# Second mixer of a two-layer backbone: eleven context copies on ScalarE, small rows ahead of the large ones, residual rows loaded late

## What is computed

```python
m = (mod_in @ mod_w[layer] + mod_b[layer])[:, None, :]
sh1, sc1, g1, sh2, sc2, g2 = jnp.split(m, 6, axis=-1)
h = modulate(rms_norm(x, norm1_g[layer]), sh1, sc1)
...
for di, rev in enumerate((False, True)):
    ...
    yc_d, h_ctx = s5_scan(u_c, lam_bar, b_bar, c_mat, h0, rev, need_ctx)
    yl_d, _ = s5_scan(u, lam_bar, b_bar, c_mat, h_ctx, rev, True)
    y = y + yl_d
...
z = jax.nn.gelu(t.reshape(t.shape[:2] + (dm,)))
val, gt = jnp.split(z @ glu_w + glu_b, 2, axis=-1)
return val * jax.nn.sigmoid(gt)
...
x = x + g1 * y
```

## Time and profile before

| | us |
|---|---|
| median of 3 runs | 2512.29 |
| lowest and highest run | 2508.5, 2512.55 |
| the profiled execution | 2506.16 |
| its span, first to last instruction | 2504.4 |

### The profile page before, as it was taken

The page is one execution under the profiler, slowest core; times in us unless marked ns, Lnnn a source line. Parts: engine busy times, 40 slices in busy tenths (PEclk is TensorE's granted clock), DMA queues, the critical chain, the costliest instruction groups (busy, mean ns, idle before and its releaser), DMA issues. The chain is left out here.

```text
span 2504.4 us, 40476 instructions
## 1 busy us (share of the span) xinstructions
PE 2143.6 (86%) x11989; PEld 1189.9 (48%) x11990; DVE 1092.3 (44%) x2311; ACT 509.8 (20%) x945; POOL 433.9 (17%) x359
## 2 busy tenths in 40 slices
PE   5889999997999999999999816699789999988874
PEld 3765444744544444444444405354444444444442
DVE  8853365944543333333333338942532222222222
ACT  3443233611121111111111125220221111100000
POOL 1000000002012222222222210000122222232332
PEclk9999999998999999999999968799799999999997
DMA  9971002003799999999999669830499999899996
GB/s 358 386 265 46 34 34 84 1 1 131 264 346 355 354 358 357 359 351 350 355 358 358 202 158 329 275 146 0 160 404 375 361 363 358 274 390 372 385 385 207
DMA packets 173622, 666.72 MB, mean 266 GB/s; under 512 B 37666, under 2 KB 48898, under 8 KB 129882
## 3 DMA queue, kind: packets, MB, share of 16 engines
q1 hardware_dynamic: 121410, 564.71, 58.7%
q0 software_dynamic: 36160, 64.84, 11.0%
q10 hardware_dynamic: 15960, 35.96, 4.1%
HBM read 617.29 MB, written 86.09 MB: 281 GB/s over the span
## 5 line engine op out<-in xcount | busy, mean ns | idle before, releaser
L1518 PE MATMUL banks_l<-slotw_l,xTw_l 128*128 128x512 f32 x800 | 358.2, 601 | 27.7 <-issue 27.7
L1529 PE MATMUL banks_l<-slotn_l,xTn_l 128*64 128x256 f32 x2816 | 325.0, 383 | 34.5 <-issue 34.5
L1529 PEld LDWEIGHTS banks_l<-slotn_l,xTn_l 128*64 128x64 f32 x2816 | 212.0, 137 | 178.9 <-issue 104.8
L1518 PEld LDWEIGHTS banks_l<-slotw_l,xTw_l 128*128 128x128 f32 x800 | 148.5, 191 | 239.3 <-issue 239.3
L1568 PE MATMUL banks_l<-slotn_l,late_l 128*64 128x512 f32 x704 | 189.9, 615 | 19.6 <-DVE late_l L1356 17.9
L1547 PE MATMUL banks_l<-slotw_l,late_l 128*128 128x512 f32 x400 | 191.8, 602 | 15.4 <-DVE late_l L1338 15.4
L977 POOL DMA_INDIRECT xgw_l<-moe_h,idxw_l x58 | 60.6, 1045 | 741.0 <-PE banks_l L1463 367.1
L1005 POOL DMA_INDIRECT moe_acc<-late_l,idxn_l x88 | 151.2, 1718 | 190.5 <-DMA moe_acc<-late_l,idxn_l 172.5
L937 POOL IOTA slotw_l<- 128x1 f32 x2 | 0.3, 140 | 729.1 <-POOLq L69 431.3
L1335 DVE TENSOR_TENSOR late_l<-late_l,banks_l 128x256 f32<-128x256 f32 x50 | 21.0, 421 | 240.2 <-ACT late_l L1107 240.2
L556 PE MATMUL ps_a<-W_a,hT_a 128*128 128x512 f32 x288 | 124.9, 595 | 0.0
(11 more groups left out here) (433 smaller groups left out, 3235.0 us busy)
## 6 DMA issues: line engine op xcount, KB each, us to landing
slotn_l<-in_exp_w_gate SPq DMA_DIRECT2D x88, 1024.0 KB
slotn_l<-in_exp_w_up SPq DMA_DIRECT2D x88, 1024.0 KB
slotn_l<-in_exp_w_down SPq DMA_DIRECT2D x88, 1024.0 KB, 12.1
slotw_l<-in_exp_w_gate SPq DMA_DIRECT2D x50, 1024.0 KB
slotw_l<-in_exp_w_up SPq DMA_DIRECT2D x50, 1024.0 KB
slotw_l<-in_exp_w_down SPq DMA_DIRECT2D x50, 1024.0 KB
w_p<-in_mod_w SPq DMA_DIRECT2D x12, 2048.0 KB, 15.4
W_a<-in_ar_w_in SPq DMA_DIRECT2D x5, 2048.0 KB, 9.4
```

The costliest lines, as they stand in the source:

```text
L1518: last = pe.matmul(pGU_w, xT_w[b % 2][:, k, :], wgu[0][b % WIDE_RING][:, :, k, :], start=(k == 0), stop=(k == KD - 1))
L1529: last = pe.matmul(pGU_n[H * side:H * side + H, b % 2], xT_n[b % 2][:, k % 4, H * (k // 4):H * (k // 4) + H], w[:, :, k, P * side:P * side ...
```

## The change

The edits are all in `s5_mixer`. Of the 16 backward context copies, ScalarE takes 11, as a third piece per half block; VectorE keeps those of `hb` 2, 5, 8, 11 and 14 (`DVE_CTX`). Sweeps and copies are no longer interleaved stage by stage: for each block VectorE does its remaining copies and then all four stages. ScalarE's queue begins with the small rows. The residual copies from `X` are gone; instead, `parts[0]` is loaded into `x` while the gated products begin, and `parts[1]` into the free lower part of `XS` (`XR`) after the last state product, and VectorE adds the two within unit 0. The three modulation buffers change places, so that the first one is free when the rows are normalised, and its load goes out there. Output weights 3 and 4 wait for two modulation products less. There are 57 memsets.

```diff
-        w = [v.rearrange("p (k n) -> p k n", k=HK) for v in (ZU[:, 0], ZU[:, 1], XS[:, SG * NCL:])]
+        w = [v.rearrange("p (k n) -> p k n", k=HK) for v in (XS[:, SG * NCL:], ZU[:, 0], ZU[:, 1])]
+        XR = XS[:, 0:NL * D].rearrange("p (m d) -> p m d", m=NL)
...
+        DVE_CTX = (2, 5, 8, 11, 14)
+
+        def evicted(hb):
+            return 3 * (hb + 1) - ctx_copied(hb)
+
+        def ctx_copied(hb):
+            return sum(k <= hb for k in DVE_CTX)
...
             for hb in range(R_ACT, NHB):
-                if hb == 4:
-                    sp.wait_ge(S['x_sum'], SL)
-                    for m in range(NL):
-                        for hh in range(2):
-                            sp.dma_start(x[hh * 64:hh * 64 + 64, m, :], X[0:64, 2 * m + hh, :]).then_inc(S['xres_in'], 16)
...
-            sp.wait_ge(S['mod_mm'], LATE)
+            sp.wait_ge(S['mod_mm'], LATE - 2)
...
+            for m in range(NL):
+                for hh in range(2):
+                    sp.dma_start(x[hh * 64:hh * 64 + 64, m, :], tile_rows(parts[0], m, hh)).then_inc(S['xres_in'], 16)
             glu_half(1)
+            sp.wait_ge(S['o_mm'], NB)
+            for m in range(NL):
+                for hh in range(2):
+                    sp.dma_start(XR[hh * 64:hh * 64 + 64, m, :], tile_rows(parts[1], m, hh)).then_inc(S['xres_in'], 16)
...
+            act.wait_ge(S['xn_done'], XN_DVE)
+            act.wait_ge(S['xn_act'], SL - XN_DVE)
+            act.dma_start(w[0], mod_weights(io, *MOD_LATE[0], 0)).then_inc(m_in[0], 16)
...
-            act.wait_ge(S['xres_in'], 16 * 8)
-            for n in range(3):
+            for n in range(1, 3):
                 act.dma_start(w[n], mod_weights(io, *MOD_LATE[n // 2], n % 2)).then_inc(m_in[n], 16)
...
+                if hb not in DVE_CTX:
+                    act.activation(VH[64:P, 0:NCC, :, gs].rearrange("p c a g -> p g a c"), v_of(hb)[64:P, :, :, 0:NCC], ACT.Copy)\
+                       .then_inc(S['va_done'], 1)
...
-            dve.wait_ge(S['xres_in'], 16 * 8)
-            for hb in range(NHB):
-                dve.wait_ge(S['va_done'], 2 * hb + 1)
-                dve.tensor_copy(VH[64:P, 0:NCC, :, 4 * hb:4 * hb + 4].rearrange("p c a g -> p g a c"), v_of(hb)[64:P, :, :, 0:NCC])\
-                   .then_inc(S['vd_done'], 1)
-                if 2 <= hb < 14:
-                    b, third = divmod(hb - 2, 3)
-                    sweep(b, third)
-                    if third == 2:
-                        sweep(b, 3)
-            for b in range(4, NB):
+            dve.wait_ge(S['xn_act'], SL - XN_DVE)
+            for b in range(NB):
+                for hb in (2 * b, 2 * b + 1):
+                    if hb in DVE_CTX:
+                        dve.wait_ge(S['va_done'], evicted(hb - 1) + 1)
+                        dve.tensor_copy(VH[64:P, 0:NCC, :, 4 * hb:4 * hb + 4].rearrange("p c a g -> p g a c"), v_of(hb)[64:P, :, :, 0:NCC])\
+                           .then_inc(S['vd_done'], 1)
                 for stage in range(4):
                     sweep(b, stage)
...
-            for _ in range(50):
+            for _ in range(57):
...
-            dve.wait_ge(S['xres_in'], 16 * 8)
...
+                if u == 0:
+                    dve.wait_ge(S['xres_in'], 16 * 16)
+                    for t in range(NL):
+                        done(dve.tensor_tensor(x[:, t, :], x[:, t, :], XR[:, t, :], ALU.add))
+                    done.wait()
...
-            pe.wait_ge(S['va_done'], 2 * NHB)
-            pe.wait_ge(S['vd_done'], NHB)
+            pe.wait_ge(S['va_done'], evicted(NHB - 1))
+            pe.wait_ge(S['vd_done'], ctx_copied(NHB - 1))
```

More of the change, by code:

```diff
@@ L2088, in s5_mixer, with tile_rows @@
         XN_DVE, R_ACT = 5, 2
+        DVE_CTX = (2, 5, 8, 11, 14)
[3 more added lines that the diff above has]
+            return sum(k <= hb for k in DVE_CTX)
+        def tile_rows(part, m, hh):
+            return part.rearrange("(m h c) d -> m h c d", m=NL, h=2)[m, hh, 0:NCL, :]
         CTX_OPS, STEPS = 4 * 4, NCL // 2 - 1
@@ L2178, in _ @@
         def _(act):
+            for s in range(2):
+                act.dma_start(vec[:, 2 * s:2 * s + 2], io['modrow'][1, s, 0:2 * D].rearrange("(a g j) -> g a j", a=2, j=SI)).then_inc(S['vec_in'], 16)
+            act.dma_start(vec[:, 4], io['norm1_g'][1].rearrange("(g j) -> g j", j=SI)).then_inc(S['vec_in'], 16)
             for j in range(2):
@@ L2181, in _ @@
                    .then_inc(x_in[j], 16)
-            for s in range(2):
-                act.dma_start(vec[:, 2 * s:2 * s + 2], io['modrow'][1, s, 0:2 * D].rearrange("(a g j) -> g a j", a=2, j=SI)).then_inc(S['vec_in'], 16)
-            act.dma_start(vec[:, 4], io['norm1_g'][1].rearrange("(g j) -> g j", j=SI)).then_inc(S['vec_in'], 16)
             act.dma_start(lam[:, 0].rearrange("p a b g -> p (a b g)"), io['s5_l8']).then_inc(S['l8_in'], 16)
@@ L2334, in sweep @@
                         dve.wait_ge(S['up'], n)
-                    dve.wait_ge(S['va_done'], 4 * (b + 1))
-                    dve.wait_ge(S['vd_done'], 2 * (b + 1))
+                    dve.wait_ge(S['va_done'], evicted(2 * b + 1))
+                    if ctx_copied(2 * b + 1):
+                        dve.wait_ge(S['vd_done'], ctx_copied(2 * b + 1))
                     dve.tensor_tensor(a, even, factor(0, 0, NPAIR, g), ALU.mult).then_inc(S['up'], 1)
@@ L2472, in _ @@
                 if hb >= 4:
-                    pe.wait_ge(S['va_done'], 2 * (hb - 3))
-                    pe.wait_ge(S['vd_done'], hb - 3)
+                    pe.wait_ge(S['va_done'], evicted(hb - 4))
+                    if ctx_copied(hb - 4):
+                        pe.wait_ge(S['vd_done'], ctx_copied(hb - 4))
                 for g in range(4):
```

## The result

| | before | after |
|---|---|---|
| median, first comparison (11 runs each) | 2505.49 | 2517.3 |
| median, second comparison (35 and 12 runs) | 2506.35 | 2512.87 |
| ratio, first comparison | | 1.0037, 95% 1.0023 to 1.0050 |
| ratio, second comparison | | 1.0029, 95% 1.0016 to 1.0042 |
| the profiled execution | 2506.16 | 2505.95 |

The ratio is not the quotient of two medians; it and its interval are what counts. The change makes the kernel slower by 0.3 to 0.4%, by the two ratios 7 to 9 us, where a gain of 0.7 us was forecast. The forecast time, 2511.6 us, and its range up to 2516.5 were set around the 2512.29 us of three runs of before; the 2505.49 of the same kernel here is 6.8 us lower.

What follows compares the result with a forecast made beforehand. VectorE's work and the DMA engines compete before the first fill, with VectorE only 2.76 us behind the last modulation product; the fill at 1605.65 against 1606.36 gave -0.7 us, 2511.6 from 2512.29, range 2506 to 2516.5.

Steps and rivals of the forecast that it cites:

- the chain from the copies to the fill: Second mixer: sweeps end 7.6 us earlier, modulation chain shifts 1.9 later, so the first fill starts at 1605.65 against 1606.36.
- Rivals 1 to 3: 1: shift 0, 2509.7, 15%; 2: modulation chain takes whole delay, 2515.1, 20%; 3: VectorE bound, 7.6 kept, 2504.7, 7%.
- I take 0.1, the end that this cover leaves, and keep 2 as the upper: Last x pair sharing turns with three V matrices: 0 to 3.1 us more, taken as 0.1, upper 2.
- The small rows' move: Head of ScalarE's queue: small rows cost the same 6 us of turns early or late, so 0 gained.
- the third pair lands as before: x loads: with the same packets ahead, the third pair isn't moved and the last sum still starts at 1493.60: 0.
- Rival 4: x loads: the last x pair loses turns, +2 us on all, 2513.6 us; chance 8%.
- The gated products keep their distance to it if TensorE catches up: After the first fill: TensorE's lag grows by 2.7 us, but it has 4.9 us to catch up over some 32.
- Cost 0; without it 2.7: Gated products behind the fill: cost 0 us if TensorE catches up, 2.7 us if it doesn't.
- ScalarE's third piece: Context copies: third piece 0.45 us like the second, group 1.77, ScalarE's total 26.1 us against VectorE's 32.45.
- the residual rows: Late loads in by 1668 to 1681, four adds of 4.9 us in unit 0 covered by VectorE's waits: cost 0.
- the relaxed wait of the output weights 3 and 4: SyncE's queue: may go after six products instead of eight, but stands behind block 7's Toeplitz load: does nothing.
- what the residual edit frees: SyncE's queue: 2 MB of copies fewer ahead of V matrices, but V products wait for VectorE's U columns: cost 0.

Runs made afterwards that it cites:

- 9: Kernel before with only the copies changed (11 of 16 on ScalarE) and output weights of blocks 5 to 7 ahead of the GLU weights: mixer 298.47 us, ratio 1.0003.
- 10: Changed kernel with x rows ahead of small rows, V matrices held until the x sums are done, GLU weights behind output weights: mixer 299.01 us, ratio 1.0002.
- 4: Changed kernel with the first half of the GLU weights behind the output weights of blocks 5 to 7: mixer 301.99 us, ratio 1.0012.
- 2: Changed kernel with small rows behind two x loads again and V matrices 4 to 6 held until all x sums are done: mixer 302.37 us, ratio 1.0019.
- 1: Changed kernel with only the small rows put back behind the first two x loads of ScalarE's queue: mixer 304.99 us, ratio 1.0029.
- 6: Kernel before with only the residual edit: late loads and adds, modulation buffers rotated, V matrices 4 to 6 not held: mixer 300.09 us, ratio 1.0011.
- 3: Kernel before with only the copies changed, 11 of 16 on ScalarE and sweeps whole: mixer 301.20 us, ratio 1.0019.

## Why the prediction was wrong

The copies' part can be read without the rest in experiments 9 and 10. Forecast times of before's trace are turned into times from its start:

| step | forecast | 9 | 10 | after |
|---|---|---|---|---|
| last x sum | +32.3 | +32.48 | +32.26 | +36.63 |
| first sweep | +62.1 | +62.13 | +61.91 | +66.29 |
| first level | +94.6 | +95.12 | +94.90 | +99.26 |
| Toeplitz block 0 | +90.9 | +91.31 | +91.10 | +95.46 |
| fourth modulation load issued | +96.6 | +96.84 | +96.68 | +100.71 |
| last modulation product ends | +144.3 | +144.01 | +144.61 | +147.53 |
| first fill | +144.4 | +144.15 | +144.75 | +147.68 |
| fill to first gated product | 39.2 | 39.19 | 39.13 | 41.95 |

**Right: the chain from the copies to the fill.** Sweeps 7.6 us earlier: the first level came 7.2 (9) and 7.4 (10) earlier. Toeplitz products 3.3 later behind the copy of group 14: in after that copy stands at 1554.24 and the first block at 1554.93. The clock had fallen by then; these are windows of after, columns as above:

```profile
1551.00:1552.00 1.00, 0.00 (x0) 0.00 (x0) 1.00 (x2) 0.94 (x2) 0.00 (x0) 0.98 0.99 418
1553.00:1554.00 1.00, 0.00 (x0) 0.00 (x0) 0.96 (x2) 0.00 (x0) 0.00 (x0) 0.50 1.03 434
```

TensorE's last V product began at 1548.25, and block and product took 5.2 us at that clock (issue of the next load at 1560.18; 5.6 in the forecast). The load's late issue cost the chain 1.9 and not 5.5: the end of the last product moved by 1.7 to 2.3. And the fill stood at -0.95 and -0.35 where -0.7 was forecast, against the product and not against VectorE, which had to wait 6.3 and 7.1 us. Rivals 1 to 3 fall with this: the delay was neither absorbed nor passed on whole, and 6.3 to 7.1 us of VectorE's gain were lost.

**Wrong: "I take 0.1, the end that this cover leaves, and keep 2 as the upper".** The last sum came 4.3 us late, and 3.0 us of it reached the mixer's end (4 against 10; 2 against after and its repetition gives 2.4 and 3.3). The step failed in three places. The small rows' move was priced at 0 by counting turns, and the count was right: by the third x sum ScalarE's queue had moved 1213 packets before and 1206 after. But turns need a start too, and the small rows moved no packet of x in the first 4 us where 64 had gone before; the stretch of the earlier trace rows lies 14 us further on and doesn't show the start. This half cost 1.2 and 1.5 us, no more than two executions of the same code differ by. That "the third pair lands as before" was wrong as well: its sum starts at +31.13 and not at +27.97. The V matrices take turns beside it too, not only beside the last pair: by then SyncE's queue had moved 1383 packets, 1120 before. Beside the last pair, the working gave 0 to 3.1 us, and the value was taken at the end where the cover hides all. VectorE's own work from the third sum to the last takes 4.4 us (1489.23 to 1493.60 before). The last pair's 192 packets need 2.6 us at 294 in 4 us and 5.0 at 155, both estimates: the cover hid most of the difference and not all. From the third sum to the last it takes 5.5 us in after, with a wait of 1.15; the five kernels without the hold (after twice, 1, 4 and 6) have 1.0 to 1.3 us more there than before. In all the V matrices' half is 1.65 alone and 2.9 in the changed kernel. Rival 4 had the last pair's part, but neither the start nor the third pair, and half the size.

**Wrong: "The gated products keep their distance to it if TensorE catches up", with "Cost 0; without it 2.7".** The distance grew by 2.6 (3) and 2.8 us (after). TensorE's spare time was counted correctly, and it did catch up: the transposes ahead of block 5's product stood 25.3 us behind the first fill in both (1631.68 before, 1632.42 after). But the argument looked only at TensorE behind the modulation chain. SyncE's queue hangs on the same chain: GLU weights, then block 5's output weights, 2.4 us later against the fill than before. Before had no slack there, and the wait and the lower clock behind it are the 2.6 to 2.8. That the prediction had 2.7 "without it" is luck: its 2.7 was the modulation chain's lag behind the fill, which TensorE did catch up; the runs showed a wait for a DMA that the working doesn't have.

**Mis-sized without effect: ScalarE's third piece**, taken at 0.45 us like the second one. Timeline of ScalarE after, half block 0 and the start of 1:

```profile
1521.31 1.07 ACT L2238 ACTIVATE UV_s<-ps_s 128x512 f32<-128x512 f32 x1 [5.35 <-PE ps_s L2501]
1522.18 0.65 ACT L2239 ACTIVATE UV_s<-ps_s 64x256 f32<-64x256 f32 x1
1522.85 0.61 ACT L2241 ACTIVATE UV_s<-ps_s 64x256 f32<-64x256 f32 x1
1523.49 1.08 ACT L2238 ACTIVATE UV_s<-ps_s 128x512 f32<-128x512 f32 x1
```

A group costs 2.18 us, not 1.77, and ScalarE worked from 1521.31 to 1552 in after without a gap, 30.7 us against 26.1. VectorE's 32.4 still hid it, by 1.7 us, and the V products ended as forecast: SyncE's output weights, which wait for the last of them, went out at +86.1 in 9 and +85.8 in 10 (before +85.9). ScalarE was all but full, though; windows of after, 1530 to 1548 (ACT 12.42 in the earlier trace rows):

```profile
1530.00:1548.00 18.00, 15.02 (x314) 14.73 (x315) 17.20 (x22) 17.68 (x27) 0.00 (x0) 0.91 0.76 224
```

**Right: the residual rows** land by 1677.26 (forecast 1668 to 1681), the four adds take 4.63 us (4.9), the wait of 11.2 us and the adds are made up for: VectorE waits for TensorE again, 4.5 us, before the unit at 1690.61. **Right: the relaxed wait of the output weights 3 and 4** does nothing: its issue comes after block 7's Toeplitz loads, as before. **Open in size: what the residual edit frees.** By itself it brings the chain's end 2.0 us earlier (6), since the V products end 1.8 earlier there and the 3 MB with them; it was costed at nothing, and is worth nothing only as long as something else ends last.

The sum, then, in steps: before 299.41, the change with its costs taken out (10) 299.01, with the x rows late (4) 301.99, with the GLU weights ahead as well (after) 304.76. That is -0.4, +3.0 and +2.8, in all 5.35 us where -0.7 was forecast. The -0.4 is smaller than the scatter of a row; that the GLU weights cost 2.7 to 2.8 comes out of two pairs of kernels (3 and 9 beside 4 and after). The range left out two costs at once, of which one was held under 2 us and the other at 0; a larger value stood beside each, 3.1 and 2.7, the second for another reason. The range's upper end lay 4.2 us above the 2512.29 it was set around. The kernel before took 6.8 us less in the comparison, so the forecast time came nearer to the measured one than the mechanism deserved.

## What to carry to other kernels

When a step is to be moved against another, list everything that hangs on the slower of the two, queues as well as engines, and ask of each how much slack it has. A wait of 0.26 us in a weight load's row, far down the list, meant that there was none: every later microsecond of that load's issue became a wait. A load that comes early for one consumer takes turns from every load beside it; hold it until the rows on the critical path have landed. Where cover is to hide a term, subtract it from the term in microseconds, and price what is left over.

## What the hardware showed

- Two queues that both have packets move equally many of them, whatever the packets' size: 369 and 368 with 0.02 and 1.44 MB in before, 155 and 154 with 0.57 and 0.54 MB after. One queue alone moves 294 in 4 us. The Trainium skill, "DMA: Bandwidth & Descriptors", section on queues, rings and completion order, states that each DMA engine goes round between the queues that have work and switches at packet boundaries. The counts here agree.
- TensorE stood still for 3.3 us ahead of the product at 1636.88, after products with gaps of up to 1 us between them. The granted clock was 1.00 through the stall and fell to 0.65 and 0.50 after the next product had begun: 1.3 us more on a 2 us product. The Trainium skill, "TensorE: Matmul & The Clock Gate", section on HAM oscillation, describes waits for DMA between short groups of products that throttle the engine each time; this row shows one such wait.
- ScalarE's copy of 64x256 takes 0.60 to 0.73 us. Followed at once by a 128x512 one in before it held the engine for 0.44 to 0.55 (twice 0.67), in the three-piece sequence of after for 0.63 to 0.70. Why the overlap goes was not tried.
